# A trunk of pooling and gated linear attention: the pooling window's chain in two channel halves, and four-column-tile matmuls undone

## The chip, the cores and the metric

The kernel runs on the 8 cores of one Trainium2 chip. Each core computes one of the eight sequences of the batch by itself, with the same program and the same weights; nothing passes between cores. The metric is the device time of the slowest core in microseconds, as a median of several executions.

## The reference

Sixteen learned meta tokens are put ahead of 2048 tokens of 1024 features, which makes L = 2064 positions. Four residual layers follow, pooling and attention in turn, then a final norm; the meta positions are dropped. Cut to what matters here:

```
def pool_mixer(h, w_in, w_grp, scale, w_out):          # layers 0 and 2
    u, z = split(h @ w_in)                             # 2048 channels each
    for gi, w in enumerate((2, 4, 8, 16)):             # 512 channels per window
        mean = (trailing sum of the last w tokens of u[gi]) / min(pos, w)
        pooled.append(mean - u[gi])
    y = einsum('blgc,gcd->blgd', pooled, w_grp)        # per group 512 x 512
    return (y * scale * silu(z)) @ w_out

def gla_mixer(h, w_in, w_gate2, b_gate, head_norm, w_out):   # layers 1 and 3
    q, k, v, z, glr = split(h @ w_in)                  # glr has 16 columns
    log_a = log_sigmoid(glr @ w_gate2 + b_gate) / 16   # forget gate, low rank
    # chunked recurrence over a state S of 256 x 512 for each of 4 heads;
    # the 16 meta tokens are a leading chunk of their own
    o = per-head RMSNorm of (masked q.k attention on v, plus q.S)
    return (o * head_norm * silu(z)) @ w_out

h = h + mixer(rmsnorm(h))                              # each layer
```

## The kernel before

All activations stay in SBUF: h in float32 (token-major, 16 tiles of 128 tokens, the meta tokens apart in hm), and hnT, the normed h transposed, in bfloat16. The work is cut into units: four channel groups of a pooling layer, in the order of the windows 8, 16, 4, 2 (GROUPS), or four heads of an attention layer. Within a unit a loop runs over nine blocks of positions (BLOCKS): block 0 of 144 (the 16 meta tokens and one tile), seven of 256 (two tiles), and a last of 128.

A pooling block has these steps. TensorE (PE) makes z and u, each as two halves k = 0, 1 of 16 matmuls into one PSUM bank (zpart, upart). ScalarE (ACT) makes sigmoid(z) in sg, VectorE (DVE) multiplies it by z into Y. ACT brings u, scaled, from PSUM to U, in which GpSimd (POOL) has put the 16 positions ahead of the block (the copy U<-U, or a memset in block 0). Since mean and matmul commute, w_grp has been multiplied into the weights of u beforehand (fold: 32 matmuls W<-W of 512 columns for the next group, in the middle of this one). Then comes window(): POOL doubles the trailing sum with shifted adds, one for window 2, two for 4, three for 8, four for 16, in turn to SA and SB from U; DVE subtracts U from the mean (scalar_tensor_tensor SB<-SB,U or SA<-SA,U) and multiplies by Y (Y<-SB,Y). At last PE multiplies Y by the output weights (outp, per tile 8 matmuls of 512 columns) and DVE adds the result to h. U, SA and SB hold all four chunks of 128 channels, 4 x 272 float32; U is there twice, Y three times. outp of a block is written behind the next block's z, u and window (pend).

The gate's low-rank projection (glr_block) and the meta tokens' values (in proj_vz, for t_ = 0) use column tiles: the eight matmuls of the contraction write to four different ranges of 32 partitions, so that the result is four partial sums; the next matmul, with its weights written four times (wg2) or keys repeated four times (ke), sums them.

The order on each engine is not the order in the code. Prog.schedule lists all operations with estimated durations, and at each step gives a free engine the ready operation that stands first in the code. What results is fixed: each engine runs its list in order, with semaphore waits. DMA issues of weights stand in POOL's list, transposes by DMA in SP's.

## Time and profile before

| | us |
|---|---|
| median of 3 executions | 1931.17 (1929.5 to 2261.3) |
| the profiled execution | 1931.17 |
| its span, slowest core | 1929.6 |
| spans of the 8 cores | 1916.6 to 1929.6 |
| PE busy | 1860.0 (96%) |
| DVE busy | 1314.8 (68%) |
| ACT busy | 1283.2 (67%) |
| POOL busy | 438.5 (23%) |

The page's shares are means over stages that differ. The first pooling layer fills about 0 to 440 us, attention follows up to about 950, then the second pooling layer up to about 1380 and the second attention. POOL works nearly in the pooling layers alone. The windows of 16 stand from about 143 to 243 and from 1084 to 1184. In all rows below, names are without buffer numbers: ps is any PSUM bank, W any weight tile.

### The profile page before, as it was taken

To read this page: it belongs to the slowest core of one execution; us is meant where nothing else is said; L and a number is where in the kernel's file an instruction comes from. 1 tells how busy PE (TensorE), PEld (TensorE's weight loads), DVE (VectorE), ACT (ScalarE), POOL (GpSimd) and SP (SyncE) were. 2 spreads that over 40 slices of the span, in tenths; PEclk is the share of its full clock that TensorE was granted. 3 is DMA by queue.
4 is the path that set the end of the run, shared out by engine and by line. 5 is a ranking of instruction groups with operands and counts; after the bars stand their busy time and mean duration, and the time that the engine had idled before them with its cause. 6 is when DMAs were issued, how large, how long until landed. Compare 5 with 4: busy or idle time off the path is not lost.

```text
span 1929.6 us, 45655 instructions; the slowest of 8 cores (1916.6 to 1929.6 us)
## 1 busy us (share of the span) xinstructions
PE 1860.0 (96%) x16072; PEld 1324.6 (69%) x16072; DVE 1314.8 (68%) x2159; ACT 1283.2 (67%) x2727; POOL 438.5 (23%) x469
## 2 busy tenths in 40 slices
PE   5999999999999999999999999999999999999997
PEld 3676767666677776777677766777667677677764
DVE  2855565686776776778765556568776767677777
ACT  4865545577666777678875554557767676767786
POOL 1649743220000000000025776332000000000000
PEclk9999999999999999999999999999999999999998
DMA  8532212534112121212442221225421121311122
GB/s 188 112 60 34 45 34 45 94 69 81 31 29 55 31 54 31 53 31 48 73 83 39 44 44 34 44 51 94 75 51 31 34 52 31 56 32 29 43 75 80
DMA packets 105536, 107.11 MB, mean 56 GB/s; under 512 B 90080, under 2 KB 92512, under 8 KB 98272
## 3 DMA queue, kind: packets, MB, share of 16 engines
q0 software_dynamic: 11856, 63.64, 18.9%
q1 hardware_dynamic: 93456, 40.56, 9.4%
q8 instruction: 131, 2.15, 0.4%
q14 instruction: 93, 0.76, 0.2%
HBM read 138.45 MB, written 8.39 MB: 76 GB/s over the span
## 4 chain that ended last, share of the span: by engine, by line
PE 85%; POOL 4%; issue 4%; DVE 3%; DMA 2%; ACT 2%; ACTq 0%; DVEq 0%; POOLq 0%; SPq 0%
PE ps L410 85%; POOL SB L449 2%; DMA W<-wpack 2%; POOL SA L449 1%; DMA hnT<-hnb 1%; DVE Y L449 1%; ACT sg L438 1%; DVE hnb L444 1%; ACT hnb L438 0%; POOL U L454 0%; DVE h L444 0%; ACT U L438 0%; DVE h L449 0%; ACT rstd L438 0%; DVE sz L444 0%
## 5 line engine op out<-in xcount | busy, mean ns | idle before, releaser
L410 PE MATMUL ps<-hnT,W 128*128 128x256 bf16 (+1 forms) x9216 | 975.1, 262 | 12.2 <-DVE sz L444 3.3
L410 PEld LDWEIGHTS ps<-hnT,W 128*128 128x128 bf16 x9216 | 825.2, 98 | 160.7 <-issue 20.0
L444 DVE SCALAR_TENSOR_TENSOR h<-ps,rs,h 128x512 f32<-128x512 f32 x256 | 191.4, 748 | 147.8 <-ACT rs L438 126.9
L410 PE MATMUL ps<-W,Y 128*128 128x512 bf16 x1024 | 247.6, 381 | 12.6 <-DVE Y L449 11.0
L449 DVE TENSOR_TENSOR h<-h,ps 128x512 f32<-128x512 f32 x256 | 175.0, 684 | 122.3 <-PE ps L410 119.5
L410 PE MATMUL ps<-W,yT 128*128 128x512 bf16 x1024 | 245.8, 382 | 0.4 <-DVE S L444 0.4
L410 PE MATMUL ps<-W,hnT 128*128 128x512 bf16 (+1 forms) x1088 | 245.3, 379 | 0.0
L454 POOL COPY el<-Eq 128x2 f32<-128x2 f32 x136 | 30.7, 226 | 817.7 <-ACT Eq L438 722.2
L444 DVE SCALAR_TENSOR_TENSOR S<-S,el,ps 128x512 f32<-128x512 f32 x240 | 178.3, 743 | 38.1 <-PE ps L410 13.0
L449 POOL TENSOR_TENSOR SA<-U 128x1080 f32<-128x1080 f32 (+7 forms) x72 | 139.3, 1935 | 285.2 <-ACT U L438 250.7
L438 ACT ACTIVATE U<-ps,vec 128x256 f32<-128x256 f32 (+2 forms) x288 | 128.9, 447 | 103.3 <-PE ps L410 79.5
L438 ACT ACTIVATE Sb<-S,el 128x512 bf16<-128x512 f32 x256 | 183.1, 715 | 15.0 <-DVE S L444 10.5
L438 ACT ACTIVATE sg<-sg 128x512 f32<-128x512 f32 (+2 forms) x288 | 168.3, 585 | 22.8 <-ACT sg L438 0.8
L438 ACT ACTIVATE gs<-gs 128x512 f32<-128x512 f32 (+2 forms) x288 | 167.5, 583 | 12.1 <-ACT gs L438 0.4
L410 PEld LDWEIGHTS ps<-W,hnT 128*128 128x128 bf16 (+1 forms) x1088 | 98.9, 98 | 107.7 <-issue 0.6
L410 PEld LDWEIGHTS ps<-W,Y 128*128 128x128 bf16 x1024 | 97.5, 98 | 107.8 <-issue 19.3
L444 DVE SCALAR_TENSOR_TENSOR sz<-ps,vec,gs 128x256 bf16<-128x256 f32 (+2 forms) x288 | 130.0, 451 | 42.2 <-ACT gs L438 31.4
L438 ACT ACTIVATE sg<-ps 128x512 f32<-128x512 f32 (+1 forms) x144 | 78.5, 545 | 117.5 <-PE ps L410 115.3
L410 PEld LDWEIGHTS ps<-W,yT 128*128 128x128 bf16 x1024 | 91.1, 97 | 92.2 <-issue 3.7
L449 DVE TENSOR_TENSOR Y<-ps,sg 128x512 bf16<-128x512 f32 (+1 forms) x144 | 90.9, 631 | 83.7 <-ACT sg L438 81.4
L438 ACT ACTIVATE Eq<-ps,nbias 128x256 f32<-128x256 f32 (+1 forms) x144 | 64.9, 450 | 123.9 <-DVE qe L444 113.8
L449 POOL TENSOR_TENSOR SB<-SA 128x1024 f32<-128x1024 f32 (+5 forms) x72 | 133.4, 1852 | 8.4 <-DVE Y L449 2.8
(83 smaller groups left out, 2138.0 us busy)
## 6 DMA issues: line engine op xcount, KB each, us to landing
W<-wpack POOLq DMA_DIRECT2D x55, 1024.0 KB, 8.6
h<-x SPq DMA_DIRECT2D x16, 512.0 KB, 5.7
out<-h SPq DMA_DIRECT2D x16, 512.0 KB, 2.7
W<-wpack POOLq DMA_DIRECT2D x10, 512.0 KB, 7.9
gbc<-gains SPq DMA_DIRECT2D x5, 512.0 KB, 5.4
kd<-ke SPq DMA_TRANSPOSE x128, 2.3
hnT<-hnb SPq DMA_TRANSPOSE x48, 3.1
wg<-wg2p POOLq DMA_DIRECT2D x8, 64.0 KB, 3.9
```

The source lines that it names most:

```text
L410: ins = e.matmul(o_, lhsT=l_, rhs=r_, start=st, stop=sp_)
L438: P.op("act", lambda e: e.activation(out=out_, in_=in_, func=func, scale=scale, **kw), reads, writes, dur, 130.0)
L444: P.op("dve", lambda e: e.scalar_tensor_tensor(out=out_, in0=a, scalar=s, in1=b, op0=op0, op1=op1), reads, writes, dve_dur(free_n(out_)) + ...
L449: P.op(eng, lambda e: e.tensor_tensor(out=out_, in0=a, in1=b, op=op), reads, writes, dve_dur(n) if eng == "dve" else n * 1.75 + 150.0, 100.0)
L454: P.op(eng, lambda e: e.tensor_copy(out=out_, in_=a), reads, writes, dve_dur(n) if eng == "dve" else n * 1.0 + 100.0, 100.0)
```

## The change

It has two parts. First, SA, SB and U become two tensors each (SA0, SA1, ...) of 2 x 272, one for each half k of the channels. In upart each half has its own copy or memset, its matmuls, its evictions and then, directly, its own window(k): all adds and both DVE operations on half the channels. Y stays one tensor of which each half writes its part. zpart now stands ahead of upart in the code in every unit, in the first one too. Second, the column tiles go: glr_block makes one product of 66 columns in eight accumulating matmuls, the meta tokens' values are eight matmuls like those of other tiles, and wg2, glrT, ke, tri and the constants lose their repeats. The core of the diff:

```
-        mm([hnTb[t_] for t_ in tiles] + [b_wglr], [bank[b]],
-           [(PS[b][32 * (kc % 4):32 * (kc % 4) + 32, 0:n], Wglr[:, kc, :], hnT[:, kc, c0:c0 + n], kc < 4, kc >= 4) for kc in range(8)], 3.0)
-        act([bank[b]], [b_glrT[bi]], glrT[:, c0:c0 + n], PS[b][:, 0:n], AF.Copy, psum=True)
+           [(PS[b][0:66, 0:n], Wglr[:, kc, :], hnT[:, kc, c0:c0 + n], kc == 0, kc == 7) for kc in range(8)])
+        act([bank[b]], [b_glrT[bi]], glrT[:, c0:c0 + n], PS[b][0:66, 0:n], AF.Copy, psum=True)
...
                 def upart():
-                    if bi == 0:
-                        P.op("pool", lambda e, U=U: e.memset(U[:, :, 0:16], 0.0), [], [A[Un]], 120.0)
-                    else:
-                        pn = BLOCKS[bi - 1][2]
-                        copy("pool", [A[Uo]], [A[Un]], U[:, :, 0:16], Up[:, :, pn:pn + 16])
                     for k in range(2):
+                        un = Un + str(k)
+                        U = T[un]
+                        if bi == 0:
+                            P.op("pool", lambda e, U=U: e.memset(U[:, :, 0:16], 0.0), [], [A[un]], 120.0)
+                        else:
+                            pn = BLOCKS[bi - 1][2]
+                            copy("pool", [A[Uo + str(k)]], [A[un]], U[:, :, 0:16], T[Uo + str(k)][:, :, pn:pn + 16])
...
-                def window():
+                        window(k, un)
+
+                def window(k, un):
...
-                        tt("pool", [A[sn]], [A[dst]], T[dst][:, :, a:e_], T[sn][:, :, a:e_], T[sn][:, :, a - d:e_ - d], ALU.add)
-                        fin = dst
+                        sn = un if src == "U" else src + str(k)
+                        dn = dst + str(k)
+                        tt("pool", [A[sn]], [A[dn]], T[dn][:, :, a:e_], T[sn][:, :, a:e_], T[sn][:, :, a - d:e_ - d], ALU.add)
+                        fin = dn
...
-                    tt("dve", [A[fin], A[Yn]], [A[Yn]], Y[:, :, 0:n], F[:, :, 16:e_], Y[:, :, 0:n], ALU.mult)
+                    tt("dve", [A[fin], A[Yn]], [A[Yn]], Y[:, 2 * k:2 * k + 2, 0:n], F[:, :, 16:e_], Y[:, 2 * k:2 * k + 2, 0:n], ALU.mult)
...
-                if ui == 0:
-                    if bi == 0:
-                        fold(0)
-                    upart()
-                    zpart()
-                else:
-                    zpart()
-                    upart()
-                window()
+                if ui == 0 and bi == 0:
+                    fold(0)
+                zpart()
+                upart()
...
-                if t_ == 0:
-                    mm(rd + [Wb[s][1]], [bank[b]],
-                       [(PS[b][32 * (kc % 4):32 * (kc % 4) + 32, :], hnT[:, kc, 0:32], Wv[:, kc, :], kc < 4, kc >= 4) for kc in range(8)], 3.0)
-                else:
-                    mm(rd + [Wb[s][1]], [bank[b]],
-                       [(PS[b][:, :], hnT[:, kc, c0 + o:c0 + o + 128], Wv[:, kc, :], kc == 0, kc == 7) for kc in range(8)])
+                mm(rd + [Wb[s][1]], [bank[b]],
+                   [(PS[b][:, :], hnT[:, kc, c0 + o:c0 + o + 128], Wv[:, kc, :], kc == 0, kc == 7) for kc in range(8)])
```

The new order on PE in the first layer's group of window 16, blocks 2 and 3. Before, from z of block 2 (W11 are the weights of z, W10 those of u, W12 those of the output; Y1 is block 1's product):

```order
L410 MATMUL ps0<-hnT,W11 128x256 x16
L410 MATMUL ps1<-hnT,W11 128x256 x16
L410 MATMUL ps7<-Y0,W12 128x16 x32
L410 MATMUL ps6<-W12,Y0 128x512 x4
L410 MATMUL ps2<-hnT,W10 128x256 x16
L410 MATMUL ps7<-W12,Y0 128x512 x4
L410 MATMUL ps3<-hnT,W10 128x256 x16
L410 MATMUL ps0<-hnT,W11 128x256 x16
L410 MATMUL ps1<-hnT,W11 128x256 x16
L410 MATMUL ps2<-hnT,W10 128x256 x16
L410 MATMUL ps6<-W12,Y1 128x512 x4
```

In the changed kernel, the same place:

```order
L410 MATMUL ps0<-hnT,W11 128x256 x16
L410 MATMUL ps7<-W12,Y0 128x512 x4
L410 MATMUL ps1<-hnT,W11 128x256 x16
L410 MATMUL ps2<-hnT,W10 128x256 x16
L410 MATMUL ps3<-hnT,W10 128x256 x16
L410 MATMUL ps0<-hnT,W11 128x256 x16
L410 MATMUL ps6<-W12,Y1 128x512 x4
L410 MATMUL ps7<-W12,Y1 128x512 x4
```

The output matmuls of block 1 stood behind both z and one half of u of block 3; now they stand between the two halves of z.

POOL in the same group, one block of 256 positions, before:

```order
L449 TENSOR_TENSOR SA<-U0 128x4x270
L454 COPY U1<-U0 128x4x16
L449 TENSOR_TENSOR SB<-SA 128x4x268
L449 TENSOR_TENSOR SA<-SB 128x4x264
L449 TENSOR_TENSOR SB<-SA 128x4x256
```

In the changed kernel:

```order
L449 TENSOR_TENSOR SA0<-U00 128x2x270
L454 COPY U10<-U00 128x2x16
L449 TENSOR_TENSOR SB0<-SA0 128x2x268
L449 TENSOR_TENSOR SA1<-U01 128x2x270
L449 TENSOR_TENSOR SA0<-SB0 128x2x264
L449 TENSOR_TENSOR SB1<-SA1 128x2x268
L449 TENSOR_TENSOR SB0<-SA0 128x2x256
L449 TENSOR_TENSOR SA1<-SB1 128x2x264
L454 COPY U11<-U01 128x2x16
L449 TENSOR_TENSOR SB1<-SA1 128x2x256
```

The adds of the two halves alternate, the second half's copy stands among them, and a DMA issue of weights would stand between such halves too.

## Rows read from the trace of the kernel before

**Rows 1.** The page's head and its part 1, busy time by engine

```profile
span 1929.6 us, 45655 instructions; the slowest of 8 cores (1916.6 to 1929.6 us)
...
PE 1860.0 (96%) x16072; PEld 1324.6 (69%) x16072; DVE 1314.8 (68%) x2159; ACT 1283.2 (67%) x2727; POOL 438.5 (23%) x469
```

**Rows 2.** Windows: busy us by engine, TensorE's clock, DMA share

```profile
0.00:50.00 50.00, 27.25 (x229) 19.78 (x230) 11.43 (x19) 25.46 (x55) 10.12 (x18) 0.97 0.87 188
143.00:243.00 100.00, 95.77 (x795) 70.43 (x793) 55.81 (x65) 53.19 (x104) 81.90 (x51) 0.98 0.25 40
243.00:440.00 197.00, 188.96 (x1612) 136.11 (x1610) 135.81 (x182) 119.74 (x263) 60.12 (x58) 0.99 0.36 62
1084.00:1184.00 100.00, 96.64 (x810) 71.56 (x808) 59.37 (x70) 53.40 (x103) 83.99 (x53) 1.00 0.23 40
```

**Rows 3.** Groups by form: count, busy us, mean ns, idle us before them

```profile
L410 PE MATMUL ps<-hnT,W 128*128 128x256 bf16 x7168 | 840.8, 273 | 8.7 <-DVE sz L444 3.3 <-DVE Y L449 3.2 <-ACT hnT L438 1.6
...
L410 PE MATMUL ps<-W,Y 128*128 128x512 bf16 x1024 | 247.6, 381 | 12.6 <-DVE Y L449 11.0 <-DVE h L449 1.3
...
L410 PE MATMUL ps<-hnT,Wglr 128*32 128x256 bf16 x112 | 5.6, 278 | 1.7 <-DMA hnT<-hnb 1.7
...
L410 PE MATMUL ps<-W,hnT 128*32 128x512 bf16 x64 | 4.9, 384 | 0.0
```

**Rows 4.** Timeline of TensorE, 377 to 384: start, duration, what, idle before

```profile
377.68 1.89 PE L410 MATMUL ps<-W,Y 128*128 128x512 bf16 x8
379.40 1.91 PE L410 MATMUL ps<-hnT,W 128*128 128x256 bf16 x16
381.15 1.89 PE L410 MATMUL ps<-W,Y 128*128 128x512 bf16 x8
382.97 0.40 PE L410 MATMUL ps<-hnT,Wglr 128*32 128x256 bf16 x8
383.30 5.41 PE L410 MATMUL ps<-hnT,W 128*128 128x256 bf16 x48
```

**Rows 5.** Timeline of GpSimd, window 16, 172 to 205

```profile
172.19 3.03 POOL L449 TENSOR_TENSOR SA<-U 128x1080 f32<-128x1080 f32 x1
175.16 1.23 POOL L454 COPY U<-U 128x64 f32<-128x64 f32 x1
176.44 1.97 POOL L449 TENSOR_TENSOR SB<-SA 128x1072 f32<-128x1072 f32 x1
178.56 1.95 POOL L449 TENSOR_TENSOR SA<-SB 128x1056 f32<-128x1056 f32 x1
180.66 2.36 POOL L449 TENSOR_TENSOR SB<-SA 128x1024 f32<-128x1024 f32 x1
183.16 3.03 POOL L449 TENSOR_TENSOR SA<-U 128x1080 f32<-128x1080 f32 x1
...
204.56 1.98 POOL L449 TENSOR_TENSOR SA<-U 128x1080 f32<-128x1080 f32 x1 [7.28 <-ACT U L438]
```

**Rows 6.** Timeline of TensorE, window 16, 187 to 219

```profile
187.41 2.82 PE L410 MATMUL ps<-W,Y 128*128 128x512 bf16 x8 [2.15 <-DVE Y L449]
...
202.99 1.89 PE L410 MATMUL ps<-W,Y 128*128 128x512 bf16 x8
...
218.67 1.89 PE L410 MATMUL ps<-W,Y 128*128 128x512 bf16 x8
```

**Rows 7.** Timeline of VectorE, window 16, 183 to 187

```profile
183.12 1.22 DVE L444 SCALAR_TENSOR_TENSOR SB<-SB,U 128x1024 f32<-128x1024 f32 x1 [3.92 <-POOL SB L449]
...
184.86 2.41 DVE L449 TENSOR_TENSOR Y<-SB,Y 128x1024 bf16<-128x1024 f32 x1
```

**Rows 8.** Timelines of GpSimd and VectorE in last blocks of 128 positions

```profile
136.43 1.07 POOL L449 TENSOR_TENSOR SB<-SA 128x528 f32<-128x528 f32 x1
...
243.34 0.69 DVE L444 SCALAR_TENSOR_TENSOR SB<-SB,U 128x512 f32<-128x512 f32 x1 [1.25 <-POOL SB L449]
```

**Rows 9.** Groups by form: the norms on VectorE

```profile
L444 DVE SCALAR_TENSOR_TENSOR hnb<-h,rstd,gbc 128x1024 bf16<-128x1024 f32 x64 | 86.9, 1362 | 38.4 <-ACT rstd L438 38.0
```

More of the change, by code:

```diff
@@ L270, in host_consts @@
 def host_consts():
-    c = np.zeros((128, 352), np.float32)
+    c = np.zeros((128, 512), np.float32)
     c[:, 0:128] = np.eye(128, dtype=np.float32)
@@ L277, in host_consts @@
             inv[g, t] = float(w) / min(t + 1, w)
-    for g in range(4):
-        c[32 * g:32 * g + 16, 256:272] = np.triu(np.ones((16, 16), np.float32))
-        c[32 * g:32 * g + 16, 336] = 1.0
-    c[:, 272:336] = inv.reshape(1, 64)
+    c[:, 256:320] = inv.reshape(1, 64)
+    c[0:16, 320] = 1.0
     return c
@@ L308, in build @@
     vecp = dt("vecp", [128, 80])
-    wglrp = dt("wglrp", [2, 128, 256])
-    wg2p = dt("wg2p", [2, 128, 1024])
-    cst = dt("cst", [128, 352])
+    wglrp = dt("wglrp", [2, 128, 8 * 66])
+    wg2p = dt("wg2p", [2, 66, 1024])
+    cst = dt("cst", [128, 512])
     out = nc.dram_tensor("out", [SEQ, D], F32, kind="ExternalOutput").ap()
@@ L336, in build @@
     msl = sb("msl", [128, 128], BF16)
-    Wglr = sb("Wglr", [128, 8, 32], BF16)
-    wg2 = sb("wg2", [128, 512], BF16)
-    glrT = sb("glrT", [128, L], BF16)
+    Wglr = sb("Wglr", [128, 8, 66], BF16)
+    wg2 = sb("wg2", [66, 512], BF16)
+    glrT = sb("glrT", [66, L], BF16)
     gbc = sb("gbc", [128, D], F32)
@@ L399, in build, with mm @@
     T = tens
-    def mm(reads, writes, lst, par=1.0):
+    def mm(reads, writes, lst):
         dur = 0.0
@@ L411, in fn @@
             return ins
-        P.op("pe", fn, reads, writes, dur / par, 170.0)
+        P.op("pe", fn, reads, writes, dur, 170.0)
     def tr(reads, writes, lst, idn):
@@ L627, in pool_layer @@
                     if bi == 3:
-                        dma("pool", "cst2", tri[:], cst[:, 128:272], [], [b_tri], 65536, after=[xs[12]])
+                        dma("pool", "cst2", tri[:], cst[:, 128:256], [], [b_tri], 65536, after=[xs[12]])
                     for b_ in {3: (0, 1), 5: (5,), 6: (6,)}.get(bi, ()) if units[1][0] % 2 == 0 else ():
@@ L740, in gla_consts @@
     def gla_consts(j):
-        dma("pool", "wglr", Wglr[:, :, :], wglrp[j].rearrange("p (kc n) -> p kc n", kc=8), [], [b_wglr], 128 * 8 * 32 * 4, after=[P.last_pe])
+        dma("pool", "wglr", Wglr[:, :, :], wglrp[j].rearrange("p (kc n) -> p kc n", kc=8), [], [b_wglr], 128 * 8 * 66 * 4, after=[P.last_pe])
         for hd in range(2):
@@ L746, in load_wg2 @@
         k = hd % 2
-        dma("pool", "wg2%d" % k, wg2[:, k * 256:(k + 1) * 256], wg2p[j][:, hd * 256:(hd + 1) * 256], [], [b_wg2[k]], 128 * 1024, after=[P.last_pe])
+        dma("pool", "wg2%d" % k, wg2[:, k * 256:(k + 1) * 256], wg2p[j][:, hd * 256:(hd + 1) * 256], [], [b_wg2[k]], 66 * 1024, after=[P.last_pe])
     class GlaLayer:
@@ L985, in build @@
     dma("sp", "vec", vec[:], vecp[:, :], [], [b_vec], 40960, after=[xs[0]])
-    dma("sp", "cst3", invw[:], cst[:, 272:344], [], [b_iw], 32768, after=[xs[0]])
+    dma("sp", "cst3", invw[:], cst[:, 256:328], [], [b_iw], 32768, after=[xs[0]])
     xs += [xload(i, [xs[0]]) for i in (2, 3)]
@@ L1050, in prep_inputs @@
         wglrp[j, :, :, 0:16] = gla_w_in[j][:, 6144:6160].reshape(8, 128, 16).transpose(1, 0, 2)
-        for g in range(4):
-            wg2p[j, 32 * g:32 * g + 16] = gla_w_gate2[j]
+        wg2p[j, 0:16] = gla_w_gate2[j]
     norms = [f(pool_norm)[0], f(gla_norm)[0], f(pool_norm)[1], f(gla_norm)[1], f(final_norm).reshape(-1)]
```

33 lines of the change are left out of this document (14 added, 19 removed).

## The prediction

> **What bounds the kernel now.** I read the page's head first, then busy time by stage, then TensorE's own timeline with the waits in it, and last GpSimd and VectorE side by side where TensorE waits. TensorE (PE) is busy 1860.0 us of 1929.6 [rows 1], so whatever adds matmul time adds wall time, and only about 70 us of waits exist to be won. The profiled execution took 1931.17 us, 1.6 more than its span, and is itself the median of the three times; the sum below is made against it.
>
> By stage [rows 2] PE idles 23 us in the first 50 (loads and first norms), 4.2 and 3.4 in the two groups of window 16 (143 to 243 and 1084 to 1184), and 8.0 in the first layer's groups of windows 4 and 2 with the passage into attention. The clock is granted at 0.97 to 1.00 of full speed there, so the loss is waiting, not clock. The reader is to see in the groups [rows 3] that waits ahead of the matmuls that read Y (the pooled product) sum to 12.6 us in the whole program, 11.0 of them for Y itself, while those ahead of the far more numerous matmuls on hnT sum to 8.7. So the split of the pooling chain can give back some 13 us at most, even if perfect.
>
> **Column tiles undone.** A tiled gate block is 8 matmuls of 128x256 that take 0.33 us from start to start, and the group ahead of it takes 1.82 where its like takes 1.72: 0.43 with the change of form [rows 4]. Untiled, 16 such matmuls take 1.75, so 8 take 0.87. That is 0.44 more for each of 14 blocks, 6.2 us; the four short blocks (144 and 128 columns, 0.50 and 0.44 untiled) add some 0.5. The meta tokens' values, 8 matmuls of 512 columns, are busy 0.61 (4.9 us in 64) against the gate block's 0.40 (5.6 in 112) [rows 3]; since the latter cost 0.43 in its place, I take 0.65. Untiled, 8 matmuls of 512 columns take 1.72 [rows 4]. That is 1.07 more for 8 heads, 8.6 us. Sum **15.3 us**. They lie where PE is the bound (the last pooling group and the attention stages), so nothing hides them. Bounds: 13, if the 1.7 us that one gate block waits for a transposed tile [rows 3] and its like absorb some; 19, if I go by busy time (0.94 against 0.40 for a gate block, 1.93 against 0.61 for the values, from the untiled groups of the same columns [rows 3]). Weights and evictions of this part keep their number, and neither queue nor eviction was late for it.
>
> The Trainium skill ("TensorEngine Tiling (Array Packing)", Tiling Modes) gives four column tiles up to four times the speed, but says that a change of tiling mode drains the engine. By four times alone the removal would cost about 20 us; the rows show two times and 2.7 times instead, drain included, so my sum stays with them.
>
> **The chain in halves: GpSimd.** In a window-16 group GpSimd (POOL) is already as busy as PE: from one SA<-U to the next are 10.97 us (172.19 to 183.16) with no gap but hand-over [rows 5], while PE needs 64 matmuls of 256 columns (4 times 1.75) and 16 of 512 (twice 1.72), 10.4 us [rows 4]. What is in the 10.97: four adds of 1.98 (the first one undisturbed, at 204.56), 1.97, 1.95 and 2.36 and a copy of some 0.23, 8.5 us; 0.45 of hand-over between dependent adds; and 2.0 us in which it stands still with VectorE (DVE). This last is to be seen in [rows 5, 7]: SA<-U starts at 183.16 beside DVE's SB<-SB,U of 1.22 and takes 3.03 where it takes 1.98 alone; DVE's Y<-SB,Y starts at 184.86, takes 2.41, twice the 1.22 of the instruction of its size before it, and ends 1.1 after POOL's add; the copy behind an add takes 1.23 (175.16), for 256 bytes in a partition. Each of the two stands still for the whole instruction of the other. The Trainium skill ("SBUF — State Buffer", SBUF: two separate sides) has this as an exclusive lock that is held for the full instruction, against a VectorE instruction with two SBUF inputs; the trace agrees (3.03 for 1.98).
>
> In halves the same elements are added by twice the instructions. An add of 1056 takes 1.95, one of 528 takes 1.07 [rows 5, 8], so 0.19 is fixed: four more adds cost 0.8. A second copy costs 0.2. The halves alternate in the new order, so the 0.45 of hand-over shrinks to about 0.15. DVE's two instructions become four of 0.69 in place of two of 1.22 [rows 7, 8], and the standing still grows with them from 2.0 to about 2.3 or, since there are now four collisions with POOL always running, 2.6. Sum 10.97 + 0.8 + 0.2 - 0.3 + 0.45 = **12.1 us a block** (11.7 to 12.6), against 10.4 of PE. POOL becomes the bound of the window-16 groups.
>
> **What PE then waits.** The order of PE matters as much. Between the last u matmul of a block and its output matmuls PE has 15.7 us of other work now (seven groups of 1.75 and 3.44 of output; in the trace 202.99 to 218.67 [rows 6]). In the changed order two of the groups stand behind: 12.2 us. When does Y come? POOL starts 1.6 after u is done (204.56) [rows 5, 6]; by halves it can start some 1.7 sooner, so at about -0.2. Adds and copies take 9.7 with hand-over, the collisions of the first half 1.3, and then the second half's DVE pair takes 0.69, a wait for the add that POOL has begun (1.1), 0.69 and some 0.25 of hand-over: Y at 13.5. Against 12.2 the first block of a run waits 1.2 and every later one the drift, 12.1 - 10.4 = 1.7. The fold of the next group (32 matmuls that wait for no Y) clears the lag in the middle, so a group has two runs of three blocks: 2 x (1.2 + 1.7 + 1.7) = 9.2, less about 0.5 because the last, short blocks relieve it: 8.7 a group, 17.4 for both. The 7.6 that both lose now goes off, so **+9.8 us**. Bounds: +2, if fold and first half hide one block in each run (the 2.15 us wait now stands right in the fold [rows 6]); +20, at 12.6 a block with no relief.
>
> **The other groups.** Window 8: three adds, 6.1 + 0.6 + 0.4 + 2.3 = 9.4 a block of POOL, under 10.4, and Y at about 11 against 12.2, so no wait. In the first layer's group, though, DVE also makes the norms (1.3 each, two a block, also of two SBUF inputs [rows 9]); that brings POOL to 12, where PE with its transposes needs 11.4: +2 (0 to 7). Windows 4 and 2 keep POOL at under 60% either way. There DVE is the busy one at the layers' ends and gets 0.3 more a block; the earlier output matmuls ask for Y sooner, while Y by halves comes sooner. The nearest row is the idle time of 243 to 440, 8.0 us [rows 2], of which the part for Y (12.6 less what the window-16 groups hold, over two layers, some 3) may go or treble: -3 to +6, and I take +1. ScalarE has the same instructions; POOL's DMA issues are the same in number (0.57 each), and stand between halves now.
>
> **Sum:** 1931.2 + 15.3 + 9.8 + 2 + 1 = **1959 us**, 1.5% slower.
>
> **Rivals.**
> - *Tiles only.* The split neither gives nor takes: the finer halves pay with latency what they cost in instructions. For it: GpSimd is idle 7.3 us behind the fold [rows 5], so a longer chain has room. Against it: PE waits for Y already at 10.97 a block. 1931 + 15 = **1947 us**.
> - *GpSimd bounds more than window 16* (slower by over 2%). At 12.6 or more a block in window 16 (both groups +20), and with halves and norms in window 8 past PE's 11.4 in the first layer (+7), and the short wait at the layers' ends doubled (+4): 1931 + 15 + 31 = **1977 us**. It decides where DVE's four short instructions meet POOL each time and DVE in turn comes late for its evictions.
> - *The split pays for the tiles* (not slower). The waits ahead of the matmuls on Y (12.6 [rows 3]) all go, because a half frees SA, SB and U sooner, and the tiles cost their lower bound: 1931 + 13 - 13 = **1931 us**. It needs POOL's period in window 16 to fall under 10.4, which four more fixed costs of 0.2 speak against; it decides only if the standing still vanishes with the shorter instructions.
> - *The halves aren't used as such.* PE reads Y as a whole and the output matmuls wait for both halves; this is so by the code, and is in the sum already.
>
> **How the numbers follow.** Forecast (1952 to 1968) 0.50; tiles only 0.20; GpSimd bounds more 0.20; the split pays 0.05; something unseen 0.05, of either sign. The range leaves out the last two and the far end of the third: **1940 to 1980**. Two per cent, about what a measurement of this kernel can tell from no change, is 1970 and 1893. Over it lie the third case and a little of the first and last: slower 0.22. Faster by 2% would need 39 us from 70 us of waits of which 23 are the start: 0.01. Within 2%: 0.77.
>
> **What would show it.** In the changed profile: gate matmuls of 66 rows at 0.87 us a block, and 8 matmuls of the meta values at 1.73; PE busy up by 15 to 19. In 143 to about 250 POOL's distance from one SA<-U of the first half to the next at about 12, without idle; DVE's half Y instructions between 0.7 and 1.8; PE's waits for Y in the window-16 groups up from 7.6 to some 17; in window 8 of the third layer none. I am wrong if POOL's distance stays under 11, if PE's idle in those groups falls, or if the wait moves to an eviction by ScalarE behind a late copy of POOL.

## The result, and the profile after

The changed kernel takes 1940.13 us (median of four) against 1930.69 of the kernel before beside it: a ratio of **1.0047, 95% interval 1.0024 to 1.0070**, some 9 us slower. Forecast were 1959 us and 1.5%. Two per cent isn't reached either way. (Single executions of 2129 and 2261 us, in which a die was disturbed, are in no ratio.) The profiled execution took 1939.16 us.

The head of its page and part 1, as in [rows 1]:

```profile
span 1937.6 us, 46392 instructions; the slowest of 8 cores (1931.2 to 1937.6 us)
...
PE 1869.6 (96%) x16072; PEld 1339.5 (69%) x16072; DVE 1379.8 (71%) x2311; ACT 1286.5 (66%) x2727; POOL 486.3 (25%) x721
```

TensorE is busy 9.6 us more, comparing core 2 with core 5, the slowest of each execution; on core 2 of both it is 14.3 (1855.3 to 1869.6). GpSimd has 252 instructions more and DVE 152. Busy time and clock in the stretches of [rows 2], core 2:

```profile
143.00:243.00 100.00, 94.42 (x786) 69.02 (x784) 70.00 (x92) 52.58 (x101) 86.36 (x98) 1.00 0.24 40
243.00:440.00 197.00, 192.16 (x1618) 141.79 (x1617) 146.13 (x217) 122.08 (x268) 65.90 (x95) 1.00 0.39 67
1084.00:1184.00 100.00, 94.51 (x791) 69.32 (x790) 68.85 (x91) 52.93 (x104) 86.49 (x97) 0.99 0.23 40
```

TensorE idles 5.6 and 5.5 us in the groups of window 16 where it idled 4.2 and 3.4, but 4.8 in windows 4 and 2 where it idled 8.0. The groups by form, as in [rows 3]; of TensorE's waits for DVE's Y, those ahead of the output matmuls fell from 11.0 to 9.8, and those ahead of matmuls on hnT rose from 3.2 to 8.7. The latter wait for a PSUM bank, which DVE frees with its product of z and sigmoid into Y:

```profile
L410 PE MATMUL ps<-hnT,W 128*128 128x256 bf16 x7168 | 838.1, 273 | 12.1 <-DVE Y L449 8.7 <-ACT hnT L438 1.6 <-ACT vb L438 1.4
...
L410 PE MATMUL ps<-W,Y 128*128 128x512 bf16 x1024 | 245.9, 379 | 12.7 <-DVE Y L449 9.8 <-DVE h L449 2.4 <-DVE SB L449 0.2
```

The gate block and the meta tokens' values without column tiles, on TensorE's timeline (start, duration, what, idle before):

```profile
376.25 1.04 PE L410 MATMUL ps<-hnT,Wglr 128*66 128x256 bf16 x8
377.12 1.91 PE L410 MATMUL ps<-hnT,W 128*128 128x256 bf16 x16
...
426.19 1.89 PE L410 MATMUL ps<-W,hnT 128*128 128x512 bf16 x8
427.92 1.89 PE L410 MATMUL ps<-W,Y 128*128 128x512 bf16 x8
```

From start to start the gate block takes 0.87 and the eight matmuls of the values 1.73, both as forecast. TensorE in the first group of window 16 (as in [rows 6]), from the first block's output on:

```profile
154.08 7.15 PE L410 MATMUL ps<-hnT,W 128*128 128x256 bf16 x64
163.10 1.89 PE L410 MATMUL ps<-W,Y 128*128 128x512 bf16 x8 [1.88 <-DVE Y L449]
...
173.54 1.89 PE L410 MATMUL ps<-W,Y 128*128 128x512 bf16 x8
...
205.09 7.15 PE L410 MATMUL ps<-hnT,W 128*128 128x256 bf16 x64
213.64 1.89 PE L410 MATMUL ps<-W,Y 128*128 128x512 bf16 x8 [1.40 <-DVE Y L449]
...
234.61 1.91 PE L410 MATMUL ps<-hnT,W 128*128 128x256 bf16 x16 [2.09 <-DVE Y L449]
```

The reader is to see that of three blocks that follow one another only the first waits (1.88 and 1.40); the second's output (173.54) finds its Y there. Last stands the wait of 2.09 behind the short blocks. Then GpSimd there, the counterpart of [rows 5], two blocks from first half to first half:

```profile
159.23 1.53 POOL L449 TENSOR_TENSOR SA<-U 128x540 f32<-128x540 f32 x1
...
171.54 1.08 POOL L449 TENSOR_TENSOR SA<-U 128x540 f32<-128x540 f32 x1 [1.42 <-ACT U L438]
172.57 0.67 POOL L454 COPY U<-U 128x32 f32<-128x32 f32 x1
173.21 1.07 POOL L449 TENSOR_TENSOR SB<-SA 128x536 f32<-128x536 f32 x1
174.24 1.08 POOL L449 TENSOR_TENSOR SA<-U 128x540 f32<-128x540 f32 x1
...
179.59 0.67 POOL L454 COPY U<-U 128x32 f32<-128x32 f32 x1
180.22 1.26 POOL L449 TENSOR_TENSOR SB<-SA 128x512 f32<-128x512 f32 x1
181.99 1.59 POOL L449 TENSOR_TENSOR SA<-U 128x540 f32<-128x540 f32 x1 [0.50 <-ACT U L438]
```

From 159.23 to 171.54 are 12.31, 1.42 of it waiting for U; from 171.54 to 181.99 are 10.45, of which 0.50 is waiting. So a block holds 10.9 and 9.9 of work, standing still included, and GpSimd waits for ScalarE's U in each: it is not the bound. DVE beside it (in [rows 7] 1.22 and 2.41 for whole instructions, 0.69 for a half alone in [rows 8]):

```profile
206.77 1.47 DVE L444 SCALAR_TENSOR_TENSOR SB<-SB,U 128x512 f32<-128x512 f32 x1
208.34 1.72 DVE L449 TENSOR_TENSOR Y<-SB,Y 128x512 bf16<-128x512 f32 x1
```

Last, a place for which I had forecast no wait, window 8 of the third layer, TensorE's waits in 990 to 1025, after, and in the second fence before (both core 2; one more of 0.30 is left out):

```profile
994.48 1.91 PE L410 MATMUL ps<-hnT,W 128*128 128x256 bf16 x16 [0.68 <-DVE Y L449]
...
1005.61 0.94 PE L410 MATMUL ps<-Y,W 128*128 128x16 bf16 x32 [2.15 <-DVE Y L449]
...
1019.90 1.89 PE L410 MATMUL ps<-W,Y 128*128 128x512 bf16 x8 [2.41 <-DVE h L449]
```

```profile
989.07 1.91 PE L410 MATMUL ps<-hnT,W 128*128 128x256 bf16 x16 [1.89 <-DVE Y L449]
```

In 995 to 1084, the stretch of this group, TensorE idles 5.6 us on core 2, where before it idled 0.0.

### The profile page after: what moved, and what is told of

The parts are those of the page before. It is cut to its first block, busy times and chain, and to the rows that moved or that the text cites. A ratio compares the mean times of both kernels' runs of the same rounds, so it can differ in the third digit from the quotient of the medians.

```text
span 1937.6 us, 46392 instructions; the slowest of 8 cores (1931.2 to 1937.6 us)
## 1 busy us (share of the span) xinstructions
PE 1869.6 (96%) x16072; PEld 1339.5 (69%) x16072; DVE 1379.8 (71%) x2311; ACT 1286.5 (66%) x2727; POOL 486.3 (25%) x721
## 3 DMA queue, kind: packets, MB, share of 16 engines
q8 instruction: 131, 2.15, 0.4%
## 4 chain that ended last, share of the span: by engine, by line
PE 83%; issue 5%; DVE 4%; ACT 4%; POOL 2%; DMA 1%; DVEq 0%; ACTq 0%; POOLq 0%; SPq 0%
PE ps L410 83%; ACT sg L438 2%; DVE Y L449 1%; DMA W<-wpack 1%; POOL SA L449 1%; POOL SB L449 1%; DMA hnT<-hnb 1%; DVE Eq L778 0%; DVE hnb L444 0%; ACT U L438 0%; ACT hnb L438 0%; DVE S L444 0%; DVE h L444 0%; DVE SB L444 0%; DVE SA L444 0%
## 5 line engine op out<-in xcount | busy, mean ns | idle before, releaser
L410 PE MATMUL ps<-W,hnT 128*128 128x512 bf16 x1088 | 256.2, 379 | 0.0
L449 POOL TENSOR_TENSOR SA<-U 128x524 f32<-128x524 f32 (+7 forms) x144 | 149.1, 1037 | 272.3 <-ACT U L438 231.7
L410 PEld LDWEIGHTS ps<-W,hnT 128*128 128x128 bf16 x1088 | 103.8, 98 | 112.8 <-issue 0.2
L438 ACT ACTIVATE gs<-gs 128x512 f32<-128x512 f32 (+2 forms) x288 | 167.7, 584 | 13.3
L449 POOL TENSOR_TENSOR SB<-SA 128x512 f32<-128x512 f32 (+6 forms) x144 | 149.8, 1047 | 2.6 <-DVE Y L449 0.4
```

The costliest lines, as they stand in the source:

```text
L410: ins = e.matmul(o_, lhsT=l_, rhs=r_, start=st, stop=sp_)
L438: P.op("act", lambda e: e.activation(out=out_, in_=in_, func=func, scale=scale, **kw), reads, writes, dur, 130.0)
L449: P.op(eng, lambda e: e.tensor_tensor(out=out_, in0=a, in1=b, op=op), reads, writes, dve_dur(n) if eng == "dve" else n * 1.75 + 150.0, 100.0)
```

## Experiments

Every kernel was timed beside the kernel before. "us" in the table is the ratio less one, times 1930.7; the intervals are about 0.1 to 0.24% wide on either side, 2 to 5 us. The six columns to its right are from the profiled executions. Marks are the starts of DVE's last residual sum of the four pooling groups, of the first head of attention and of the last; a column has the time from the mark before it to its own, as a difference to the kernel before (433.0, 140.8, 421.8, 370.8, 141.4, 409.2 us), median of the eight cores. L1 is the first pooling layer with the attention behind it, L3 the second pooling layer with its attention. "Price" is what the planner's list of costs has for an add on GpSimd, against the kernel before.

| kernel | tiles | halves | price | ratio, 95% interval | us | L1 pool | L1 head 1 | L1 heads 2-4 | L3 pool | L3 head 1 | L3 heads 2-4 |
|---|---|---|---|---|---|---|---|---|---|---|---|
| after | off | all | 1 | 1.0047 (1.0024-1.0070) | +9.1 | -5.3 | +4.9 | +1.4 | +5.8 | +3.2 | +0.6 |
| split_only | on | all | 1 | 1.0004 (0.9994-1.0013) | +0.8 | -7.0 | +1.6 | +0.3 | +5.3 | -0.1 | +0.4 |
| tiles_off | off | none | 1 | 1.0043 (1.0026-1.0059) | +8.3 | -1.8 | +4.9 | +1.8 | 0.0 | +3.6 | +0.9 |
| gate_off | values on | none | 1 | 1.0053 (1.0036-1.0069) | +10.2 | -3.1 | +6.9 | +0.1 | -0.9 | +7.2 | +0.5 |
| tiles_same | off | none | 1 | 1.0074 (1.0062-1.0086) | +14.3 | +1.3 | +2.1 | +3.2 | +3.8 | +2.1 | +2.3 |
| adds_halved | on | adds | 1 | 0.9999 (0.9990-1.0009) | -0.2 | -10.4 | +9.2 | -0.2 | -4.0 | +6.0 | -0.3 |
| dve_halved | on | DVE's | 1 | 1.0045 (1.0030-1.0060) | +8.7 | +2.0 | +0.4 | +0.6 | +6.5 | -0.9 | -0.1 |
| adds_8_16 | on | adds, w 8, 16 | 1 | 0.9956 (0.9939-0.9972) | -8.5 | -4.1 | -0.4 | +0.3 | -2.4 | -0.4 | 0.0 |
| split_16 | on | all, w 16 | 1 | 1.0043 (1.0027-1.0059) | +8.3 | +4.1 | -0.4 | +0.4 | +2.0 | -0.1 | +0.7 |
| split_2_4 | on | all, w 4, 2 | 1 | 0.9995 (0.9974-1.0017) | -1.0 | -4.3 | +1.6 | +1.4 | 0.0 | -0.1 | +0.7 |
| before_cost | on | none | 1.15 | 0.9991 (0.9982-1.0000) | -1.7 | -4.2 | +2.7 | +0.4 | -0.1 | -0.4 | -0.8 |
| split_c107 | on | all | 1.07 | 0.9993 (0.9972-1.0014) | -1.4 | -6.7 | +1.4 | +0.3 | +3.5 | -0.1 | -0.8 |
| **split_cost** | on | all | 1.15 | **0.9938 (0.9925-0.9951)** | **-12.0** | -9.4 | +1.4 | +0.2 | -1.9 | -0.1 | -0.2 |
| split_c120 | on | all | 1.20 | 0.9984 (0.9960-1.0008) | -3.1 | -4.9 | +1.4 | +0.3 | +0.7 | -0.1 | 0.0 |
| split_c130 | on | all | 1.30 | 1.0033 (1.0021-1.0046) | +6.4 | -0.4 | +1.7 | +0.2 | +6.4 | -0.1 | +0.1 |
| split_priced | on | all | 1.06, DVE too | 1.0038 (1.0025-1.0051) | +7.3 | -5.2 | +8.9 | +0.3 | +2.2 | +0.3 | -0.7 |
| adds_cost | on | adds | 1.15 | 0.9970 (0.9951-0.9989) | -5.8 | -8.3 | +4.5 | +0.3 | -2.9 | +0.2 | -0.1 |
| adds816_cost | on | adds, w 8, 16 | 1.15 | 1.0007 (0.9998-1.0015) | +1.4 | -3.7 | +3.8 | +0.4 | -0.3 | -0.4 | +0.3 |
| after_cost | off | all | 1.15 | 1.0001 (0.9979-1.0024) | +0.2 | -9.7 | +4.9 | +1.6 | +1.0 | +1.2 | +1.0 |

### Each part alone

**split_only** has the hunks of upart, window and the buffers, **tiles_off** all the others.

> The kernel before with the pooling chain in halves, its column tiles kept. Theory A (the tiles' removal cost its 15 us in full, the split costs nothing in the window-16 groups and takes some waits and clock losses away elsewhere): 15 less than the changed kernel, 1924 to 1928, ratio to before 0.996 to 0.999. Rival B (the tiles were worth only some 5 us, the split costs 5): 1934 to 1937, ratio 1.002 to 1.004. On A, GpSimd's busy stretch in window 16 shows 9.9 to 10.9 us a block, on B and as predicted 12.

> The kernel before with only the column tiles removed, the pooling chain whole. Theory A: 1930.7 + 15 = 1944 to 1948, ratio 1.007 to 1.009. Rival B: 1934 to 1938, ratio 1.002 to 1.004. In its trace a gate block of 256 columns takes 0.87 us on TensorE and the meta tokens' values 1.73 on either theory; on B the time would come back in a wait behind them.

Measured: +0.8 and +8.3 us, which add up to the 9.1 of the change. Both terms of the prediction were put too high, the split by some 12 us and the tiles by 7. Neither theory of the two expectations came: 1931.7 for split_only lies between A and B, and so does tiles_off with 1939.

### Which halves

**adds_halved** keeps DVE's two instructions whole, behind the second half's adds; **dve_halved** is the reverse, all adds whole:

```
# adds_halved
-                        tt("pool", [A[sn]], [A[dst]], T[dst][:, :, a:e_], T[sn][:, :, a:e_], T[sn][:, :, a - d:e_ - d], ALU.add)
+                        tt("pool", [A[sn]], [A[dn]], T[dn][:, :, a:e_], T[sn][:, :, a:e_], T[sn][:, :, a - d:e_ - d], ALU.add)
+                    if k == 0:
+                        return
+                    stt(bf + bu, bf, F[:, :, 16:e_], F[:, :, 16:e_], 1.0 / w, U4[:, :, 16:e_], ALU.mult, ALU.subtract)
# dve_halved
+                    for q in range(2):
+                        stt([bf, A[Un + str(q)]], [bf], F[:, :, 16:e_], F[:, :, 16:e_], 1.0 / w, T[Un + str(q)][:, :, 16:e_], ALU.mult, ALU.subtract)
+                        tt("dve", [bf, A[Yn]], [A[Yn]], Y[:, 2 * q:2 * q + 2, 0:n], F[:, :, 16:e_], Y[:, 2 * q:2 * q + 2, 0:n], ALU.mult)
```

> Column tiles kept. GpSimd's adds and copies in halves as in the split, VectorE's two instructions on the whole block. If the short hold of VectorE's instructions is what keeps GpSimd from standing still, the block in window 16 now takes about 11 (8.95 of adds, 0.4 of copies, 2.0 of standing still, less the overlap of instructions without dependence) and the time is 3 to 6 us above split_only. If what counts is that alternating halves hand over without a gap, it is 10 to 10.5 and within 2 us of split_only.

> Column tiles kept. GpSimd's adds on the whole block as before, VectorE's two instructions in halves. If the short hold is what counts: standing still falls from 2.0 to 1.0 to 1.4 and the block in window 16 takes 10.0 to 10.4, time as split_only. If the hand-over counts, the block stays at 10.9 to 11.3 and the time at the kernel before or up to 4 us over it.

Measured: -0.2 and +8.7. In window 16 a block of adds_halved takes GpSimd 11.3 us (158.10 to 169.37), of which it waits 1.3 for U: 10.0 of work, as the theory of the hand-over has it. In dve_halved it takes 11.7 (163.94 to 175.67), 1.3 of it waiting until DVE has read SB for both halves. DVE's halves alone cost; that it is these waits and the added instructions, and not the order, which changed too, is not shown. The halved adds alone gain 10.4 and 4.0 us in the pooling groups and lose 9.2 and 6.0 in the first head of attention. Of the 9.2, 5.67 are one wait. TensorE and ScalarE of adds_halved there, and the sync engine's queue, in which transposing DMAs stand one behind the other (a row goes from the issue of its first DMA to the end of the last one's issue, gaps included):

```profile
439.27 0.25 PE L422 MATMUL ps<-o,ones 128*128 128x16 bf16 x4 [5.67 <-DVE yT L461]
```

```profile
434.95 1.06 ACT L450 ACTIVATE hnb<-h 128x1024 bf16<-128x1024 f32 x1 [7.69 <-DMA hnT<-hnb]
```

```profile
423.30 10.42 SPq L435 DMA_TRANSPOSE hnT<-hnb  x2
```

```profile
423.12 0.57 POOL L470 DMA_DIRECT2D W<-wpack  x1 [5.51 <-PE ps L422]
```

Read from below: the load of 1 MB of weights is issued at 423.12 and two transposes behind it, at 423.30 and 425.87; ScalarE's square of the next tile waits 7.69 for the buffer that the first transpose reads, DVE's norm waits for ScalarE, DVE's yT stands behind the norm in its queue, and TensorE waits 5.67 for yT. From issue to landing (the last number) the load and the first transpose take, and then the same transpose of split_cost (below), issued at 422.44, ahead of the load at 425.00:

```profile
W<-wpack POOLq DMA_DIRECT2D x1, 1024.0 KB, 10.9
hnT<-hnb SPq DMA_TRANSPOSE x1, 11.6
```

```profile
hnT<-hnb SPq DMA_TRANSPOSE x1, 3.1
```

Behind the load the transpose lands at 434.87, just after the load (434.04). This is not peculiar to the place: on core 2 of the kernel before, 49 of 176 transposes are issued while a load of weights is under way, and all 49 land after that load, 6.0 us from issue on the median against 2.3 for the other 127; in the changed kernel it is 44 of 44, in adds_halved and in split_cost 49 of 49. No run moved the load alone, but what the order decides here is which transposes stand behind a load.

### Which groups, which tiles

**adds_8_16** halves the adds for windows 8 and 16 only, **split_16** and **split_2_4** take the whole split for these windows only; the other groups are whole, on the same buffers. **gate_off** undoes the column tiles of glr_block alone.

```
+FULL, ADDS = (), (8, 16)          # (16,), ()   and   (2, 4), ()
+                mode = "full" if w in FULL else "adds" if w in ADDS else "whole"
...
+                if mode == "whole":
+                    window(1, Un)
```

> The column tiles kept; the adds of the window and the copies in halves, DVE's two instructions whole, in the groups of window 8 and 16 alone (z ahead of u there); the groups of window 4 and 2 as before. Theory A: the gain of the halved adds lies in windows 8 and 16 (2.6 and 6.3 in the first layer, 3.2 and 3.2 in the third, by the halved adds in all groups) and its loss (9.2 and 6.0 in the first heads of attention, with the shifts of windows 4 and 2 8.5 for each passage) is made by the halves in windows 4 and 2, whose adds are short anyway. Then some 1916 to 1920, 0.6 to 0.8% faster. Rival B: the loss comes of the gain itself: whoever reaches the passage into attention some 9 us sooner meets a transposing DMA or a weight load at another point there and waits for it, so the first heads lose 5 to 9 again here: 1928 to 1931. To be seen in TensorE's wait for yT near 431 (5.7 with halved adds everywhere, none before).

> The column tiles kept; adds and DVE's instructions in halves in the group of window 16 alone, everything else whole as before. Theory A (gains are local to window 16): 5.9 in the first layer and 2.7 in the third, 1931 - 8.6 = 1922.5, 0.45% faster. Rival B (given back at the passage): 1928 to 1931. Rival C, that of the prediction (GpSimd bounds the group at 12.1 a block): 1931 + 9.8 = 1941, which the two runs of the whole split already speak against.

> The column tiles kept; adds and DVE's instructions in halves in the groups of window 4 and 2 alone. Theory A: the split loses 2.5 and 3.4 from window 4 to the first head of attention in the two layers, where the adds are short and DVE is the busy one: 1931 + 6 = 1937, 0.3% slower. Rival B: these groups lose only when the ones before them gained, so no difference here, 1931 to 1932.

> The gate projection alone without column tiles (66 rows, 16 matmuls' worth in 8 of one tile), the meta tokens' values still in four column tiles; no split. Theory A: a gate block costs its 0.43 more, but half of the 14 blocks stand where TensorE waits for a late transposed tile anyway, so 1931 + 3 to 4 = 1934.5; the values cost the other 4 to 5 of the 8.3 of both together. Rival B: the gate blocks cost all of their 6.7 (1938) and the values, in whose heads TensorE waits for the state anyway, 1.6.

Measured: -8.5, +8.3, -1.0 and +10.2. adds_8_16 is faster, without the wait at the passage, but by less than the sum of its groups. split_16 overturns my reading: the same instructions in window 16 as in split_only, and 8 us slower, not faster. I had taken the start of the 64th residual sum as the end of window 16, which moves with the order of the outputs and made gains out of shifts; over all four groups the table has them right. And gate_off alone (10.2, interval 7.0 to 13.3) costs no less than gate and values together (8.3, 5.0 to 11.4), where 6.7 was its price. Neither fits a theory of prices that add. What differs is the order. TensorE at the fold (W into PSUM) of split_16 and of split_only:

```profile
178.56 1.91 PE L425 MATMUL ps<-hnT,W 128*128 128x256 bf16 x16
180.30 1.89 PE L425 MATMUL ps<-W 128*128 128x512 bf16 x7
186.35 3.41 PE L425 MATMUL ps<-W,Y 128*128 128x512 bf16 x8 [4.16 <-DVE Y L464]
```

```profile
177.36 3.66 PE L412 MATMUL ps<-hnT,W 128*128 128x256 bf16 x32
180.85 2.18 PE L412 MATMUL ps<-W 128*128 128x512 bf16 x8
182.90 1.89 PE L412 MATMUL ps<-W,Y 128*128 128x512 bf16 x8
```

In split_only 32 matmuls and 8 of the fold stand ahead of the output, which then doesn't wait; in split_16 it is 16 and 8, and TensorE waits 4.16 us for Y. One group is 1.75 of that. More is in DVE's queue, split_16 and then split_only:

```profile
180.21 1.73 DVE L464 TENSOR_TENSOR Y<-SB,Y 128x512 bf16<-128x512 f32 x1
181.87 1.47 DVE L464 TENSOR_TENSOR h<-h,ps 128x512 f32<-128x512 f32 x2
183.25 1.47 DVE L459 SCALAR_TENSOR_TENSOR SB<-SB,U 128x512 f32<-128x512 f32 x1
```

```profile
180.58 0.68 DVE L446 SCALAR_TENSOR_TENSOR SB<-SB,U 128x512 f32<-128x512 f32 x1
```

In split_16 two residual sums (h<-h,ps) stand ahead of the second half's SB<-SB,U, which starts at 183.25, 3.0 after the first half's product; in split_only it starts at 180.58. The code of that block is the same in both; the planner's times have come out otherwise since window 8, and it put the output sooner on one engine and the chain's end later on another.

### The order held, and the order moved

**tiles_same** is tiles_off with the planner told the old costs for the untiled matmuls and the small DMAs, so that every engine has the order of the kernel before, row for row. **split_cost**, **adds816_cost** and **before_cost** are split_only, adds_8_16 and the kernel before with one number changed in the planner, and with it nothing that an engine does but its order:

```
# tiles_same
+           [(PS[b][0:66, 0:n], Wglr[:, kc, :], hnT[:, kc, c0:c0 + n], kc == 0, kc == 7) for kc in range(8)], 3.0)
+                   [(PS[b][:, :], hnT[:, kc, c0 + o:c0 + o + 128], Wv[:, kc, :], kc == 0, kc == 7) for kc in range(8)], 3.0 if t_ == 0 else 1.0)
# split_cost, adds816_cost, before_cost
-             dve_dur(n) if eng == "dve" else n * 1.75 + 150.0, 100.0)
+             dve_dur(n) if eng == "dve" else (n * 1.75 + 150.0) * 1.15, 100.0)
```

> The column tiles undone as in the change, no split, but the planner still costs the gate blocks and the values of tile 0 at a third, as before: every engine's order is then that of the kernel before, row for row. Theory A: a gate block costs its 0.43 and the values their 1.07 wherever TensorE has no wait behind them, and the two totals so far (8.3 for both, 10.2 for the gate alone) differ from 15.3 because the planner, told of the longer matmuls, changed the order of the passage into attention, once for the better and once for the worse. With the order held, 1931 + 12 to 15 = 1943 to 1946. Rival B: the waits that follow in the same heads absorb the longer matmuls whatever the order: 1931 + 8 = 1939 again.

> Column tiles kept, the chain in halves in every group, and the planner's cost of an add on GpSimd 1.15 times what it was (1.23 for a half where the trace shows 1.07 to 1.5 beside VectorE). Nothing that an engine does is changed by it but the order. Theory A (the halves gain, and TensorE's order, which asks for Y before it is there by what the planner doesn't know of the standing still, eats it): TensorE's waits for Y fall from 22 to some 10 us, 1931 - 8 = 1923, 0.4% faster. Rival B (the chain itself is what is waited for): the waits stay, 1929 to 1933.

> Column tiles kept, adds in halves for windows 8 and 16 alone, planner's cost of an add times 1.15. Theory A: its waits for Y go too, 1923 - 4 = 1919. Rival B: no less than the 1923 of the same kernel at the old cost; or slower, where a group moved behind an output makes the residual sums and so the norms late at the passage into attention: 1926.

> The kernel before with nothing but the planner's cost of an add times 1.15. Theory A (order counts for as much as the chain): its 14 us of waits for Y fall by some 5, 1926. Rival B: without halves GpSimd's 10.97 a block against TensorE's 10.4 set the pace of window 16 and a later output only moves the wait: 1930 to 1932.

Measured: +14.3, -12.0, +1.4 and -1.7. With the order held the tiles cost what the sum said: 14.3 (12.0 to 16.6) against tiles_off's 8.3, by the same matmuls in another order. On the mean of the six cores of each profiled execution that have all 16072 matmul records, TensorE is busy 14.8 us more than before in tiles_off, 7.8 in gate_off and 16.6 in tiles_same, and idle 3.3 less, 3.2 more and 0.8 less. So the longer matmuls are paid for in every order; the waits differ, and between tiles_same and tiles_off also the clock (1.8 us). split_cost is the fastest kernel of the study, 0.6% under the kernel before. TensorE in its window 16, against the rows of after above:

```profile
151.77 10.64 PE L412 MATMUL ps<-hnT,W 128*128 128x256 bf16 x96
162.25 1.89 PE L412 MATMUL ps<-W,Y 128*128 128x512 bf16 x8
...
201.36 8.90 PE L412 MATMUL ps<-hnT,W 128*128 128x256 bf16 x80
210.09 1.89 PE L412 MATMUL ps<-W,Y 128*128 128x512 bf16 x8
...
221.77 1.89 PE L412 MATMUL ps<-W,Y 128*128 128x512 bf16 x8 [1.00 <-DVE Y L451]
```

Six groups (96 matmuls) where after has four stand ahead of the first output, five where it has four ahead of the later one, and the waits of 1.88 and 1.40 are gone; the longest that is left is one of 1.00 at the short blocks. Over the whole program, core 2, TensorE's waits for DVE's Y are 13.7 us, where split_only has 20.9 and the kernel before 14.2; what it gains on the kernel before lies more in other waits, for DVE's h (2.8 to 0.5) and for weights (6.6 to 5.0). The stretch 143 to 250 of split_cost and then of the kernel before (behind the stretch its length, then PE's busy time):

```profile
143.00:250.00 107.00, 103.94 (x882) 76.01 (x881) 74.00 (x104) 54.16 (x108) 88.81 (x101) 1.00 0.30 52
```

```profile
143.00:250.00 107.00, 101.62 (x850) 74.63 (x848) 64.33 (x76) 57.10 (x110) 88.99 (x58) 1.00 0.25 43
```

Idle are 3.1 against 5.4 before (and 5.2 against 6.5 in 250 to 440, 1.8 against 3.8 in 50 to 143). Without the halves the same price gains 1.7 (before_cost), and with halved adds in two groups it takes 10 us away (adds816_cost against adds_8_16): it is no remedy in itself.

### One kind order, or the true price?

The planner's DVE half costs 0.65 us, where the groups by form of after have 0.96 to 0.99 for SB<-SB,U and SA<-SA,U and 1.20 for Y<-SB,Y (0.83 for Y<-SA,Y of windows 8 and 2); its add in window 16 is priced 1.08 on the mean, where it takes 1.14 (1.07 to 1.22 by form). So 8 x 0.06 + 0.32 + 0.55, some 1.4 us of the way to Y in a block of window 16, are missing in the model, and 1.15 on eight adds gives 1.3 of it. **split_c107**, **split_c120** and **split_c130** take other factors, **split_priced** the prices measured in window 16, for all groups, **adds_cost** and **after_cost** 1.15 on other kernels:

```
# split_priced
                     stt([A[fin], A[un]], [A[fin]], F[:, :, 16:e_], F[:, :, 16:e_], 1.0 / w, T[un][:, :, 16:e_], ALU.mult, ALU.subtract)
+                    P.ops[-1].dur *= 1.5
                     tt("dve", [A[fin], A[Yn]], [A[Yn]], Y[:, 2 * k:2 * k + 2, 0:n], F[:, :, 16:e_], Y[:, 2 * k:2 * k + 2, 0:n], ALU.mult)
+                    P.ops[-1].dur *= 1.8
...
+             dve_dur(n) if eng == "dve" else (n * 1.75 + 150.0) * 1.06, 100.0)
```

> As the split with the planner's add at 1.15 times its cost, with 1.07 in its place. Theory A (outputs stand where the modelled Y is due, and the true chain is about 1.15 times the modelled one): between the two, waits for Y near 17 us, 1925. Rival B (any change of order moves the time by some us either way, by chance): anywhere between 1915 and 1935, with the difference in other waits than those for Y.

> The same with 1.30. Theory A: TensorE's waits for Y stay at 14 us or less, and window 16 keeps its gain; what is lost is at the ends of groups, where late outputs make the residual sums late: 1918 to 1922. Rival B as for 1.07: 1915 to 1935, in other waits than for Y.

> Adds in halves in all groups, DVE's two instructions whole, planner's cost of an add 1.15. Theory A (the halves of the adds are what helps and DVE's two further fixed costs only cost): as fast as the split at that cost or faster, 1915 to 1919, unless the 5.7 us wait of the first head of attention (a transposing DMA beside a weight load) is met again. Rival B: DVE's halves matter since the first half of Y's product lies beside the second half's adds: 1922 to 1925.

> The whole change, tiles undone and chain split, with the planner's add at 1.15. Theory A (the two parts add): 1918.8 + 8.3 = 1927, or + 14 = 1933 where the order is not kind to the longer gate blocks. Rival B: the gain of the split with that cost was luck of one order, and here it is gone: 1938 to 1945.

> The split alone, the planner's costs set to what the trace shows in window 16: an add times 1.06, DVE's SB<-SB,U half times 1.5 (0.98 for 0.65), its Y<-SB,Y half times 1.8 (1.2). Theory A (the order is good when the prices are true): 1917 to 1922, as at 1.15. Rival B (1.15 was one kind order): 1925 to 1938.

> The split alone with an add at 1.20 of its cost. Theory A: near 1.15's 1918.8, up to 1924 on the way to 1.30's 1937.9. Rival B: anywhere from 1919 to 1938, above 1925 as likely as below.

Measured, against the kernel before: -1.4, +6.4, -5.8, +0.2, +7.3 and -3.1. From 1.00 to 1.30 the split stands at +0.8, -1.4, -12.0, -3.1, +6.4: a hollow with one deep point. The prices of window 16 give +7.3, with 8.9 lost again in the first head of attention. TensorE there:

```profile
435.55 0.63 PE L412 MATMUL ps<-vb,kd 128*128 128x512 bf16 x1 [5.21 <-DMA kd<-ke]
```

A weight load is issued at 424.85 in this kernel and lands at 434.70, and the transposes of ke that are issued behind it, at 425.72 and 426.93, land at 435.04 and 435.21; TensorE waits until 435.55, at the passage that adds_halved showed. In split_c130 TensorE waits for ScalarE's U instead (2.11 and 2.12 at 168.43 and 181.15), with u groups moved next to each other. So the theory that true prices give good orders is not borne out, as far as these prices are true (Y<-SA,Y is now priced 1.18 and takes 0.83); 1.15 is to a good part one kind order. What stays: after_cost, the change as made with that one number, runs level with the kernel before, 9 us ahead of the change, and 12 behind split_cost, which is what the untiled matmuls cost between these two orders.

## Why the prediction was wrong, step by step

**What bounds the kernel** was read rightly: TensorE is at 96% before and after. On the mean of the six cores with all matmul records it is busy 13.5 us more after the change and idle 1.7 less, where 15.3 and 12.8 more were forecast. So the matmuls came nearly as priced, with 3.8 us less lost to the clock, and the waits did not. (I had named 15 to 19 more busy time as a sign; on core 2 of both executions it is 14.3.)

**Column tiles, 15.3.** Price and count were right (0.87 and 1.73 in their places; 14.3 measured with the order held). The step that failed is "They lie where PE is the bound [...], so nothing hides them", since it takes the waits around them as given. The planner was told of the longer matmuls and reordered the passage into attention: tiles_off paid 14.8 more in matmul time, waited 3.3 less and cost 8.3; gate_off, with less untiled, waited 3.2 more and cost 10.2. That the same untiled matmuls cost 14.3 in the old order shows that the new order gave the 6 us back. The lower bound of 13 was too high for what the change does, and right for what the matmuls take.

**GpSimd's period of 12.1 in window 16** was the central step, and it failed: 10.9 and 9.9 us of work, and 9.5 in the first block (149.69 to 159.23). (1) Bare work was put at 9.5 (8.5 + 0.8 + 0.2) and hand-over at 0.15; by the rows of after six adds take 1.03 from start to start (173.21 to 174.24), the last add of each half 1.23, and a copy 0.2 where nothing disturbs it, 9.0 in all. The kernel before has 8.9 with its hand-over (8.5 + 0.45), so the four added adds and the copy cost 0.1 and not 0.7: the halves alternate and overlap. (2) Standing still was put at 2.45: in 171.54 to 181.99 it is two copies of 0.67 for 0.20, 0.9; in the block before it, 1.9. I had argued that each engine stands still for the other's whole instruction; by halves DVE bears much of it (1.47 and 1.72 for 0.69, each started 0.15 and 0.12 after an add of GpSimd, 206.62 and 208.22). The Trainium skill ("SBUF — State Buffer", SBUF: two separate sides) has an exclusive lock held for the full instruction by whichever starts first; these rows agree (DVE waits 0.78 and 1.03), while GpSimd loses less than DVE's 0.69 each time (0.47 for a copy). The sign that I named, a distance under 11, came half: 12.3 and 10.5, with 1.4 and 0.5 of it idle.

**What PE then waits, +9.8.** Waits of 1.2, 1.7 and 1.7 in each run of three blocks were forecast; 1.88 or 1.40, 0 and 0 came, and 2.09 with the short blocks that I had as relief. In the stretches of window 16 idle time went from 7.6 to 11.1, not to 17. That the first output comes too soon (12.2 against 13.5) was right; the drift was not, since GpSimd, with time to wait for U in every block, keeps pace.

**The other groups, +3.** Windows 4 and 2 of the first layer: idle 8.0 to 4.8, a gain of 3.2, just past my bound of -3 and not at the +1 that I took. Window 8 of the first layer: the added instructions beside the norms cost nothing (idle in 50 to 143 on core 2 is 2.9, before 3.8; forecast were 2 more). Window 8 of the third layer, for which I wrote "so no wait": 0.68, 2.15 and 2.41 where one of 1.89 stood, and 5.6 us of idle time in 995 to 1084 where there was none. In split_only the pooling groups of the third layer give back 5.3 of the first layer's 7.0. I argued from GpSimd's period only, and there the first Y of the group is asked for sooner than any period decides.

**Rivals.** "Tiles only" had the right mechanism for the split (latency given and taken) with 1947; with the tiles at 8.3 it is the result. "GpSimd bounds more" is out: it waits for U. "The split pays for the tiles" was given 0.05 and said to need a period under 10.4; the work of a block came to 9.5 to 10.9, and only in another order, after_cost, is the time level with the kernel before. The range's lower end, 1940, lies at the measured 1940.1; that it holds the result is luck, since of its two large terms one was not there and the other was half given back.

**What stays open.** That a weight load makes the 5 to 6 us wait at the passage rests on the landing times, and on no run that moves only the load. Why 1.15 is so much better than 1.07 and 1.20 was not followed further than to the waits.

## What to carry to other kernels

Where a program orders instructions by a cost list, the price of an edit is two terms: what it takes with the order held, which the trace gives well (15.3 against 14.3 here), and what the new order does, which here was -13 to +10 us (split_cost against split_only, adds816_cost against adds_8_16). Ask for each moved instruction what stands between it and its consumer in the in-order queue, and run the edit once with the old costs and once with two others before judging it. Splitting a chain whose steps depend on one another removes the hand-over between them, so charge it the fixed cost of the added instructions less all of that (here 8.9 to 9.0 us of bare work a block); ask which transfers stand behind a large load; and mark stages by something whose place in the order the edit can't move.
